# Reordering the two MLP products of a float32 transformer block on one core: DVE's other work between the splits, slices with their high and low parts in one piece each

## The chip, the core and the metric

The kernel runs on one core of one Trainium2 chip. The metric is device time in microseconds (us): the median of three runs, with a profile of one further execution. TensorE (PE) multiplies, VectorE (DVE) and ScalarE (ACT) prepare its operands and finish its results, SyncE (SP) issues most loads, GpSimd (Pool) issues the transfers that add in memory. SP, ACT and Pool each have a DMA queue; in the profile they are q1, q10 and q0.

## What is computed

One layer of a streaming encoder in float32: RMSNorm, an input projection, two kinds of attention, gates, an output projection, and then an MLP of hidden width 8192 for 512 tokens of width 2048. The change is in the MLP alone:

```
h2 = rms_norm(x, norm_mlp[layer])
u = jax.nn.relu(h2 @ w_mlp_up[layer])
x = x + (u * u) @ w_mlp_down[layer]
```

## The kernel before

**Numbers in two parts.** A float32 operand is split into a high part, rounded to PE's fast float32 format (ACT, an activation with Copy), and a low part, the rest (DVE, a subtraction). A product is three matmuls: high by high, high by low, low by high.

**Seven products instead of eight.** Both MLP products multiply 2 x 2 blocks by a scheme of the Strassen and Winograd kind with seven products. DVE first makes sums of blocks of weights (L1425, L1428, L1430, one call `sum_pairs` for the weights of two units), and combines the seven results afterwards (`combine_early`, L1445 to L1451, and `combine_late`, L1458) once ACT has copied one of them (`copy_p1`, L892).

**Units.** A unit is two slices of activations by a pair of weight tiles: 2 x 7 x 3 = 42 matmuls. It needs the weights' high part (`round_pair`, ACT L887) and low part (`split_pair`, DVE L1435). There are two buffers for these parts, so `round_pair` of unit n waits until PE has finished unit n - 2. Four weight buffers `pairs[0..3]` hold raw weights and sums.

**The up product** has 32 pairs of columns p, four units each. A loop over i takes two pairs: m = 0 to 3 is one, m = 4 to 7 the next, with the results in two sets of PSUM banks. The results of one pair are combined at m = 1 or m = 5 of the next. ACT then squares them (`finish_pair`), DVE makes the sums that the down product needs (`sum_u`, L1677 to L1683), and ACT stores them as one row block of `u_rows` in device memory, seven tiles of 256 columns (`store_u`).

**The down product** has 32 groups g of four units j = 0 to 3: eight column blocks by four windows of the hidden width. Group g uses the eight slices g to g + 7, of which each next group exchanges one; slice e lies in buffer e modulo 8. `load_slice` brings it back (SP, L601), `round_slice` (ACT, L1119) and `split_slice` (DVE, L1722) split it. The loads, as SP issues them:

```
for g in range(GROUPS):
    for j in range(4):
        load_down(g, j)          # waits until pair_lo_ready says that buffer j is free
        ...
        if g > 0 and j == 1 and g + 7 < EVENTS:
            load_slice(g + 7)
```

PE waits before every unit for `pair_lo_ready` (the split of the weights), and in the down product for `slice_ready` of the slices up to g + 2j + 1. For the first 24 groups Pool stores the combined results into `sum_rows` (from the ninth group on with addition). In the last eight (`CLOSING` = 24 and up) DVE adds the stored sums (`total`), PE transposes ahead of unit j = 3 of the next group (`turn_out`, L2119), ACT scales from PSUM into `out_tok` (`scale_out`, four activations, L1126), and Pool adds `out_tok` to the output in memory (`add_out`). `scale_out` waits until `out_tok` is free again, `at_least(act, out_added, 16 * (g - CLOSING))`, and PE's group g + 2 waits for `scale_out` of g.

**Order.** Each engine runs its own list, written out by hand; semaphores tie the lists together. A waiting instruction holds up everything behind it on its engine. In `up_pairs` and in the loops over g, each engine's list says in which place of a unit a side task stands; the change is mostly about these places. On DVE, before: at unit 1 (and 5) `combine_early`, `split_pair`, `combine_late`; after `split_pair` of each even unit the next `sum_pairs`. On ACT, before: at unit 1 (and 5) `copy_p1` and then `round_pair`.

**Slices in SBUF.** A slice buffer is 7 tiles x 2 parts x 256 columns: high and low part of a tile stand side by side. The load fills the low part's place, in seven pieces of 1 KB per row, and both parts are then made from there. The up product uses the same buffers for its eight slices of the normed input.

## Time and profile before

| | us |
|---|---|
| median of 3 runs | 2810.18 |
| lowest, highest | 2807.93, 2812.83 |
| the profiled execution | 2803.63 |
| its span, first to last instruction | 2801.9 |
| PE busy in the span | 2677.7 |
| DVE busy | 1990.3 |
| ACT busy | 1204.7 |
| mean granted TensorE clock | 0.993 of full speed |

The up product runs from 1350 us to 2038 us of the span, the down product from 2044 us to 2784 us. PE is counted busy while a matmul is under way, so the difference to a stretch's length is time in which PE had nothing to do. L numbers are lines of the kernel.

### The profile page before, as it was taken

To read this page: it belongs to the slowest core of one execution; us is meant where nothing else is said; L and a number is where in the kernel's file an instruction comes from. 1 tells how busy PE (TensorE), PEld (TensorE's weight loads), DVE (VectorE), ACT (ScalarE), POOL (GpSimd) and SP (SyncE) were. 2 spreads that over 40 slices of the span, in tenths; PEclk is the share of its full clock that TensorE was granted. 3 is DMA by queue.
4 is the path that set the end of the run, shared out by engine and by line. 5 is a ranking of instruction groups with operands and counts; after the bars stand their busy time and mean duration, and the time that the engine had idled before them with its cause. 6 is when DMAs were issued, how large, how long until landed. Compare 5 with 4: busy or idle time off the path is not lost.

```text
span 2801.9 us, 48322 instructions
## 1 busy us (share of the span) xinstructions
PE 2677.7 (96%) x18330; PEld 2484.5 (89%) x18330; DVE 1990.3 (71%) x3081; ACT 1204.7 (43%) x1539; POOL 74.2 (3%) x100
## 2 busy tenths in 40 slices
PE   9999999999999999999999999999979989988997
PEld 8999999888888888888999999999979988888897
DVE  4558886777777644434777787777788777777775
ACT  5534444555554532233444444444453333333443
POOL 0000000000010000000000000000000000000000
PEclk9999999999999999999999999999989999999999
DMA  6444444333233254434344444443474555555564
GB/s 242 125 124 136 127 135 123 84 83 79 75 79 82 84 144 138 144 125 158 111 137 137 150 137 143 136 151 131 149 230 157 167 148 155 159 159 154 170 175 104
DMA packets 396462, 381.43 MB, mean 136 GB/s; under 512 B 18368, under 2 KB 380480, under 8 KB 395840
## 3 DMA queue, kind: packets, MB, share of 16 engines
q1 hardware_dynamic: 366352, 311.73, 36.6%
q10 hardware_dynamic: 21168, 47.19, 4.5%
q0 software_dynamic: 8832, 20.97, 4.0%
q8 instruction: 77, 1.26, 0.2%
q14 instruction: 33, 0.27, 0.0%
HBM read 316.91 MB, written 62.91 MB: 136 GB/s over the span
## 4 chain that ended last, share of the span: by engine, by line
PE 56%; DVE 20%; DMA 11%; issue 6%; ACT 5%; SPq 1%; ACTq 0%; DVEq 0%; POOL 0%
DMA h<-u_rows 8%; DVE lo L1435 7%; PE job L1777 7%; PE job L1780 7%; PE job L1779 7%; ACT hi L887 3%; DVE pair L1425 3%; DVE h L1722 2%; DMA pair<-in_w_mlp_up 2%; DVE pair L1428 2%; ACT h L1119 2%; DVE blocks L1445 1%; PE heads_out L1877 1%; PE job L2090 1%; DVE pair L1430 1%
## 5 line engine op out<-in xcount | busy, mean ns | idle before, releaser
L887 ACT ACTIVATE hi<-pair 128x1792 fp32r<-128x1792 f32 x270 | 458.5, 1698 | 600.1 <-PE wide L2094 269.3
L1435 DVE TENSOR_TENSOR lo<-pair,hi 128x1792 fp32r<-128x1792 f32 x270 | 545.8, 2022 | 141.0 <-ACT hi L887 140.9
L2090 PE MATMUL scores<-h,hi 128*128 128x256 f32 x1024 | 297.2, 290 | 62.9 <-DVE lo L1435 62.9
L2090 PE MATMUL job<-h,hi 128*128 128x256 f32 x1024 | 294.1, 287 | 41.7 <-DVE lo L1435 41.7
L722 ACT ACTIVATE w_hi<-raw 128x512 fp32r<-128x512 f32 x268 | 168.8, 631 | 353.9 <-PE job L1780 242.9
L1175 DVE TENSOR_TENSOR w_lo<-raw,w_hi 128x512 fp32r<-128x512 f32 x268 | 187.1, 699 | 158.2 <-ACT w_hi L722 157.2
L2094 PE MATMUL scores<-h,lo 128*128 128x256 f32 x1024 | 291.8, 285 | 0.0
L2092 PE MATMUL scores<-h,hi 128*128 128x256 f32 x1024 | 291.5, 285 | 0.0
L2094 PE MATMUL job<-h,lo 128*128 128x256 f32 x1024 | 290.0, 283 | 0.0
L2092 PE MATMUL job<-h,hi 128*128 128x256 f32 x1024 | 289.9, 283 | 0.0
L2090 PEld LDWEIGHTS scores<-h,hi 128*128 128x128 f32 x1024 | 197.9, 193 | 71.7 <-issue 47.7
L2090 PEld LDWEIGHTS job<-h,hi 128*128 128x128 f32 x1024 | 196.3, 192 | 50.3 <-issue 40.0
L1777 PE MATMUL job<-a_hi,w_hi 128*128 128x512 f32 x560 | 229.5, 410 | 0.0
L1780 PE MATMUL job<-a_hi,w_lo 128*128 128x512 f32 x560 | 219.6, 392 | 0.0
L1779 PE MATMUL job<-a_lo,w_hi 128*128 128x512 f32 x560 | 218.6, 390 | 0.0
L1425 DVE TENSOR_TENSOR pair<-pair 128x1024 f32<-128x1024 f32 x128 | 156.5, 1222 | 82.4 <-DMA pair<-in_w_mlp_down 57.5
L2092 PEld LDWEIGHTS scores<-h,hi 128*128 128x128 f32 x1024 | 198.1, 194 | 0.0
L2094 PEld LDWEIGHTS scores<-h,lo 128*128 128x128 f32 x1024 | 198.1, 193 | 0.0
L2094 PEld LDWEIGHTS job<-h,lo 128*128 128x128 f32 x1024 | 196.5, 192 | 0.0
L2092 PEld LDWEIGHTS job<-h,hi 128*128 128x128 f32 x1024 | 196.5, 192 | 0.0
L2090 PE MATMUL turned<-h,hi 128*128 128x256 f32 x512 | 146.0, 285 | 0.0
L2092 PE MATMUL turned<-h,hi 128*128 128x256 f32 x512 | 146.0, 285 | 0.0
(458 smaller groups left out, 7025.8 us busy)
## 6 DMA issues: line engine op xcount, KB each, us to landing
pair<-in_w_mlp_up SPq DMA_DIRECT2D x256, 256.0 KB, 2.8
pair<-in_w_mlp_down SPq DMA_DIRECT2D x248, 256.0 KB, 3.3
raw<-in_w_in SPq DMA_DIRECT2D x79, 512.0 KB, 4.1
h<-u_rows SPq DMA_DIRECT2D x39, 896.0 KB, 9.0
u_rows<-u_blocks ACTq DMA_DIRECT2D x32, 896.0 KB, 4.1
pair<-in_w_gate SPq DMA_DIRECT2D x84, 256.0 KB, 2.9
raw<-in_w_out SPq DMA_DIRECT2D x64, 256.0 KB, 3.3
sum_rows<-blocks POOLq DMA_DIRECT2D x24, 512.0 KB, 7.4
```

What stands on the lines that cost most here:

```text
L722: nc.scalar.activation(into, raw[:, slot, part:part + KU], ACT.Copy).then_inc(hi_ready, 1)
L887: nc.scalar.activation(pair_hi[j % 2], pairs[j][:, :, 1:8], ACT.Copy).then_inc(pair_hi_ready, 1)
L1119: nc.scalar.activation(slot[:, :, 0], slot[:, :, 1].bitcast(F32), ACT.Copy).then_inc(slice_hi, 1)
L1175: nc.vector.tensor_tensor(lo, raw[:, slot, part:part + KU], hi.bitcast(F32), ALU.subtract).then_inc(split_ready, 1)
L1425: nc.vector.tensor_tensor(t[:, :, 4:6], t[:, :, 1:3], t[:, :, 0:1].broadcast_to([P, 4, 2, P]), ALU.add).then_inc(sums_first, 2)
L1435: nc.vector.tensor_tensor(pair_lo[j % 2], pairs[j][:, :, 1:8], pair_hi[j % 2].bitcast(F32), ALU.subtract).then_inc(pair_lo_ready, 1)
L1777: nc.tensor.matmul(result[:, :], high[:, k], act_hi[:, f], start=(n == 0 and k == 0), stop=False)
L1779: nc.tensor.matmul(result[:, :], high[:, k], act_lo[:, f], start=False, stop=False)
L1780: done = nc.tensor.matmul(result[:, :], low[:, k], act_hi[:, f], start=False, stop=(n == units - 1 and k == KU - 1))
L2090: nc.tensor.matmul(into, high, h_slices[s][:, a, 0], start=first, stop=False, skip_group_check=True)
L2092: nc.tensor.matmul(into, high, h_slices[s][:, a, 1], start=False, stop=False, skip_group_check=True)
L2094: done = nc.tensor.matmul(into, low, h_slices[s][:, a, 0], start=False, stop=(j == 3 and k == 1), skip_group_check=True)
```

## The change

DVE and ACT do their side tasks in another place: at each unit the split of weights (and ACT's rounding for it) comes first, and then one other task. In the down product the slices' buffers are seen as two contiguous parts, high and low, through `slots`, and PE reads them through `down_slice`; the load then writes one piece of 7 KB per row. The up product keeps the old layout. In the first group the splits of slices 4 to 7 stand one place later than before, one or two at a time. `scale_out` of a group moves from unit 3 of the group after it to unit 0 of the one after that, behind `round_pair`.

```diff
             out_tok = over(third, "out_tok", [P, TB, 2 * P])
+
+        slots = [[t.rearrange("p a l s -> p (a l s)")[:, 7 * 2 * P * l:7 * 2 * P * (l + 1)] for l in range(2)]
+                 for t in h_slices]
+
+        def down_slice(e, a, l):
+
+            return slots[e % 8][l][:, 2 * P * a:2 * P * (a + 1)]
...
                 sp.wait_ge(u_stored, 16 * (e % PAIRS + 1))
-                sp.dma_start(h_slices[e % 8][:, :, 1].bitcast(F32),
-                             u_rows[e % PAIRS].rearrange("p (a s) -> p a s", a=7)).then_inc(slice_loaded[e % 8], 16)
+                sp.dma_start(slots[e % 8][1].bitcast(F32), u_rows[e % PAIRS]).then_inc(slice_loaded[e % 8], 16)
...
                     n = i * 8 + (GU + m)
-                    if m == 0 and not first:
-                        store_u(i * 2 - 2)
+                    if not (first and m < 4):
+                        round_pair(n, m % 4, n - 1)
                     if m == 1 and not first:
...
                         copy_p1(i * 2 + GP, 0, blocks)
-                    if not (first and m < 4):
-                        round_pair(n, m % 4, n - 1)
+                    if m == 0 and not first:
+                        store_u(i * 2 - 2)
                     if m == 2 and not first:
...
                 act.wait_ge(slice_loaded[e % 8], 16 * (e // 8 + 1))
-                slot = h_slices[e % 8]
-                nc.scalar.activation(slot[:, :, 0], slot[:, :, 1].bitcast(F32), ACT.Copy).then_inc(slice_hi, 1)
+                hi, lo = slots[e % 8]
+                nc.scalar.activation(hi, lo.bitcast(F32), ACT.Copy).then_inc(slice_hi, 1)
...
                     n = down_unit(g, j)
+                    round_pair(n, j, n - 1)
+                    if j == 0:
+                        if g < 2:
+                            store_u(PAIRS - 2 + g)
+                        if g == CLOSING + 2:
+                            act.wait_ge(r2_ready, 1)
+                            act.wait_ge(u_stored, 16 * PAIRS)
+                        if g >= CLOSING + 2:
+                            scale_out(g - 2)
                     if j == 1:
...
                         copy_p1(GP + PAIRS + g - 1, (g - 1) % 2, blocks)
-                    round_pair(n, j, n - 1)
                     if g == 0 and j == 0:
-                        store_u(PAIRS - 2)
-                    if g == 0 and j < 3:
-                        round_slice(2 * j + 2)
-                        round_slice(2 * j + 3)
+                        round_slice(2)
+                        round_slice(3)
+                    if g == 0 and j == 1:
+                        round_slice(4)
+                        round_slice(5)
                     if g == 0 and j == 2:
                         finish_pair(PAIRS - 1)
-                    if g == 1 and j == 0:
-                        store_u(PAIRS - 1)
-                    if j == 3:
-                        if g + 8 < EVENTS:
-                            round_slice(g + 8)
-                        if g == CLOSING:
-                            act.wait_ge(r2_ready, 1)
-                            act.wait_ge(u_stored, 16 * PAIRS)
-                        if g > CLOSING:
-                            scale_out(g - 1)
+                        round_slice(6)
+                        round_slice(7)
+                    if j == 3 and g + 8 < EVENTS:
+                        round_slice(g + 8)
             act.wait_ge(total_ready, GROUPS - 1 - CLOSING)
             copy_p1(GP + PAIRS + GROUPS - 1, (GROUPS - 1) % 2, blocks)
+            scale_out(GROUPS - 2)
             scale_out(GROUPS - 1)
...
                         continue
+                    split_pair(n, m % 4)
                     if m == 1:
                         combine_early(i * 2 + (GP - 1), 1, blocks)
+                        combine_late(i * 2 + (GP - 1), 1, blocks)
                     if m == 5:
                         combine_early(i * 2 + GP, 0, blocks)
-                    split_pair(n, m % 4)
-                    if m == 1:
-                        combine_late(i * 2 + (GP - 1), 1, blocks)
-                    if m == 5:
                         combine_late(i * 2 + GP, 0, blocks)
...
                 dve.wait_ge(slice_hi, e + 1)
-                slot = h_slices[e % 8]
-                nc.vector.tensor_tensor(slot[:, :, 1], slot[:, :, 1].bitcast(F32), slot[:, :, 0].bitcast(F32),
-                                        ALU.subtract).then_inc(slice_ready, 1)
+                hi, lo = slots[e % 8]
+                nc.vector.tensor_tensor(lo, lo.bitcast(F32), hi.bitcast(F32), ALU.subtract).then_inc(slice_ready, 1)
...
                     n = down_unit(g, j)
+                    split_pair(n, j)
+                    if g == 0 and j == 1:
+                        split_slice(4)
                     if j == 1:
                         combine_early(p, (g - 1) % 2, blocks)
-                    split_pair(n, j)
-                    if j == 1:
                         combine_late(p, (g - 1) % 2, blocks)
...
                             total(g - 1)
-                    if g == 0 and j < 3:
-                        split_slice(2 * j + 2)
-                        split_slice(2 * j + 3)
+                    if g == 0 and j == 2:
+                        split_slice(5)
                     if j % 2 == 0 and n + 2 < down_unit(GROUPS, 0):
                         sum_pairs(n + 2, (j + 2) % 4)
-                    if j == 3:
-                        if g == 0:
-                            sum_u(PAIRS - 1)
-                        if g + 8 < EVENTS:
-                            split_slice(g + 8)
+                    if g == 0 and j == 0:
+                        split_slice(2)
+                        split_slice(3)
+                    if g == 0 and j == 3:
+                        split_slice(6)
+                        split_slice(7)
+                        sum_u(PAIRS - 1)
+                    if j == 3 and g + 8 < EVENTS:
+                        split_slice(g + 8)
             combine_early(GP + PAIRS + GROUPS - 1, (GROUPS - 1) % 2, blocks)
...
-            def up_unit(n, j, b, slices_wait=False, at=0):
+            def up_slice(s, a, l):
+
+                return h_slices[s][:, a, l]
+
+            def up_unit(n, j, b, slices_wait=False, at=0, slice_of=up_slice):
...
                 for k in range(2):
-                    s = (at + 2 * j + k) % 8
+                    s = at + 2 * j + k
                     if slices_wait:
...
                         first = j == 0 and k == 0 and half == 0
-                        nc.tensor.matmul(into, high, h_slices[s][:, a, 0], start=first, stop=False,
+                        nc.tensor.matmul(into, high, slice_of(s, a, 0), start=first, stop=False,
                                          skip_group_check=True)
-                        nc.tensor.matmul(into, high, h_slices[s][:, a, 1], start=False, stop=False,
+                        nc.tensor.matmul(into, high, slice_of(s, a, 1), start=False, stop=False,
                                          skip_group_check=True)
-                        done = nc.tensor.matmul(into, low, h_slices[s][:, a, 0], start=False,
+                        done = nc.tensor.matmul(into, low, slice_of(s, a, 0), start=False,
                                                 stop=(j == 3 and k == 1), skip_group_check=True)
...
                     pe.wait_ge(slice_ready, g + 2 * j + 2)
-                    up_unit(down_unit(g, j), j, g % 2, at=g)
+                    up_unit(down_unit(g, j), j, g % 2, at=g, slice_of=down_slice)
             turn_out(GROUPS - 1)
```

## Rows read from the trace of the kernel before

**Rows 1.** Busy time by stage: stretch, us, PE PEld DVE ACT POOL (instructions), PEclk, DMA, GB/s
```profile
1397.30:1995.50 598.20, 572.42 (x4706) 566.52 (x4704) 472.43 (x505) 257.86 (x224) 0.00 (x0) 1.00 0.42 141
1995.50:2099.30 103.80, 87.45 (x671) 86.16 (x670) 85.22 (x81) 50.99 (x39) 0.78 (x1) 0.92 0.62 201
2099.30:2599.40 500.10, 455.11 (x3703) 447.76 (x3701) 380.57 (x354) 191.46 (x134) 16.63 (x22) 1.00 0.55 157
2599.40:2784.30 184.90, 170.76 (x1400) 168.15 (x1400) 141.21 (x138) 76.24 (x73) 14.37 (x16) 1.00 0.59 159
```

**Rows 2.** The chain that ended last, up product: start us, us, what
```profile
1619.20 0.12 PE scores L2094
```

**Rows 3.** Who waited for whom, PE, whole span: us, times, longest us
```profile
PE scores L2090 <- DVE lo L1435: 62.9, 43, 6.2
PE job L2090 <- DVE lo L1435: 41.7, 47, 3.3
```

**Rows 4.** Timeline of ACT, up product: start us, us, what [idle before]
```profile
1611.48 1.69 ACT L887 ACTIVATE hi<-pair 128x1792 fp32r<-128x1792 f32 x1
```

**Rows 5.** Timeline of DVE in the same pair, columns as above
```profile
1613.56 0.69 DVE L1445 TENSOR_TENSOR blocks<-job,blocks 128x512 f32<-128x512 f32 x1
...
1615.55 2.01 DVE L1435 TENSOR_TENSOR lo<-pair,hi 128x1792 fp32r<-128x1792 f32 x1
```

**Rows 6.** Timeline of PE in the same pair
```profile
1617.62 0.39 PE L2090 MATMUL scores<-h,hi 128*128 128x256 f32 x1 [1.36 <-DVE lo L1435]
```

**Rows 7.** The chain that ended last, one down group
```profile
2305.30 1.95 DVE lo L1435
...
2308.24 9.95 DMA h<-u_rows
...
2318.22 1.71 ACT h L1119
...
2319.95 1.65 DVE h L1722
...
2321.89 2.02 DVE lo L1435
...
2328.63 1.94 DVE lo L1435
```

**Rows 8.** DMA queues: packets, MB, share; q1 and q10 from 1500 to 2000, q0 from 2100 to 2600
```profile
q1 hardware_dynamic: 51099, 49.26, 31.4%
q10 hardware_dynamic: 3456, 22.02, 10.6%
...
q0 software_dynamic: 3168, 11.54, 12.5%
```

**Rows 9.** Landings: u_rows 2110:2740 and 1500:2000, in_w_mlp_down 2110:2740, out_tok 2640:2802
```profile
DMA to landing us min/median/max: 7.0/9.1/11.2
...
DMA to landing us min/median/max: 4.0/4.1/4.2
...
DMA to landing us min/median/max: 2.3/3.4/10.6
...
DMA to landing us min/median/max: 5.6/5.9/8.2
```

**Rows 10.** Timeline of Pool, the down group of rows 7
```profile
2307.86 0.85 POOL L676 DMA_DIRECT2D sum_rows<-blocks  x1 [22.79 <-DVE blocks L1458]
```

**Rows 11.** Timeline of ACT at the end
```profile
2784.57 0.38 ACT L892 ACTIVATE blocks<-heads_out 128x256 f32<-128x256 f32 x1 [3.51 <-PE heads_out L2094]
2790.49 1.57 ACT L1126 ACTIVATE out_tok<-job,r 128x256 f32<-128x256 f32 x4 [5.54 <-PE job L2119]
```

**Rows 12.** The chain that ended last, a transposing in the last groups
```profile
2778.57 0.87 PE scores L2119 x8
```

**Rows 13.** Timeline of DVE, first down group
```profile
2048.72 2.03 DVE L1722 TENSOR_TENSOR h<-h 128x1792 fp32r<-128x1792 f32 x1 [2.65 <-ACT h L1119]
```

**Rows 14.** Timeline of PE, first down group
```profile
2072.21 0.36 PE L2090 MATMUL scores<-h,hi 128*128 128x256 f32 x1 [2.28 <-DVE lo L1435]
```

## The prediction

> **What bounds the kernel now.** I read the stages' busy time first, then who waited for whom, then one period of each MLP product on DVE, ACT and PE and as a chain of waits, then the DMA queues and the times to landing.
>
> The stages [rows 1]: the up product's steady part is 28 pairs of columns in 598.2 us, so 21.36 us a pair; the down product's steady part is 22 groups in 500.1 us, 22.7 us a group; the last eight groups take 184.9 us. A pair and a group are both four units of 42 matmuls (two slices, seven products, three matmuls each). The chain steps through them at 0.12 us a matmul [rows 2]: 5.04 us a unit, 20.2 us for four. PE's busy time per up pair is 572.42 / 28 = 20.4 us, which still holds a slow first matmul after each wait. I take 20.3 us as what four units cost when PE never waits. PE is then the bound only in part: 1.1 us of each pair and 2.4 us of each group are waits, and PE waits for one thing in both products, the DVE split of the weights: 62.9 + 41.7 us over the kernel [rows 3].
>
> Why that split is late differs. In the up product ACT has the high part of unit m = 1 from 1611.48 to 1613.17 [rows 4], but DVE, done with its sums at 1613.56, first does the whole of combine_early (L1445 to L1451), so the split starts at 1615.55 [rows 5] and PE waits 1.36 us until 1617.62 [rows 6]. In the down product the same stands before unit j = 1, and a longer loop runs through it [rows 7]: the split of j = 1 ends (2307.25), SP issues two weight loads and then the slice (2308.24), the slice lands 9.95 us later, ACT rounds it, DVE splits it, then splits j = 0, then sums, combines, splits j = 1 (2328.63 + 1.94 = 2330.57). From one such end to the next are 23.3 us. Written as a sum: 1.0 to the issue, L to the landing, 1.73 ACT, 1.94 slice split, 2.02 split of j = 0, 4.72 for sums and combine_early (2321.89 + 2.02 = 2323.91 to 2328.63), 1.94 split. That is 13.35 + L, with L = 9.95 it is 23.3, the measured period. So this loop, and not PE, sets the down product.
>
> **The change, part by part.**
> 1. *The split of unit 1 (and 5) goes ahead of combine_early, and ACT's rounding ahead of copy_p1.* Nothing is added; combine_early is 2.0 us of DVE (1613.56 to 1615.55) [rows 5], copy_p1 a short copy on ACT. Take PE's start of the unit before as 0. ACT's high part is ready at 1.9 us (released by the end of the unit before that), the sums (2.75 us, 4.72 of rows 7 less the combine's 2.0) end at 1.6 if the split ahead of them ended 1.1 us early, the split runs to 3.95, ahead of 5.04. Then both combines (2.4 us) to 6.3, where unit 2's high part comes at 6.9; its split ends at 8.9 of 10.1. Every slot holds one split (1.95 from start to start) and at most the sums: 4.7 of 5.07 us. So in the up product PE's wait should go: 598.2 - 28 x 20.3 = 29.8 us. What hides the combine is the 15 us before its bank is needed again.
> 2. *The same in the down product.* It takes the combine out of the loop: 11.3 + L. This is under 20.3 as long as L is under 9.0 us.
> 3. *High and low part of a slice each in one piece.* The matmuls read the same 256 columns. ACT's and DVE's durations shouldn't change: the weights' split and the slice's split take 2.02 us for the same 1792 elements in different pieces [rows 7] (the 1.65 us there is the part on the chain; the next instruction's start shows 1.94). I give them nothing; both bounds are 0. What changes is the transfer: rows of 7 KB instead of seven pieces of 1 KB. From 1500 to 2000 us q1, all 1 KB pieces, spent 31.4% of 16 x 500 us on 49.26 MB, 51 engine-us per MB; q10, which stores whole slices, 10.6% on 22.02 MB, 38.5 per MB [rows 8]. A slice of 0.9175 MB would need 2.2 us of all engines instead of 2.9. Bounds of L: 4.1 us, what the store of a slice takes, and 9.1 (7.0 to 11.2), what the load takes now [rows 9]. One more thing pulls it down. Pool's store of the sums leaves at 2307.86 [rows 10], 0.4 us ahead of the slice, and costs 12.5% of 8000 engine-us per 11.54 MB, so 2.8 us of all engines for its 0.52 MB [rows 8]. It waits for the combine. With the 2.0 us of combine_early behind the split it leaves 2.6 us after the split's end, the slice 1.0, so 1.6 us ahead. Two weight loads (0.52 MB at 51, 1.7 us) stay ahead: 1.7 + 2.2 + 1.9 (4.1 less 2.2) = 5.8, and some sharing. I take L = 6.5. Then the loop is 17.8 us, under 20.3, and PE bounds the down product: 500.1 - 22 x 20.3 = 53.5 us saved.
> 4. *scale_out after the next round_pair, one group later.* In the last eight groups the rounding of j = 0 stood behind four activations of 1.57 us together [rows 11]; now they stand behind it, with PE's unit j = 3 to cover them. PE's own floor is 8 x 20.3 + 7 x 0.9 (the transposes [rows 12]) = 168.7 of 184.9 us: 16.2 us saved. total adds two instructions of 512 elements, some 1.2 us, to DVE's slot of j = 1, 1.95 + 2.4 + 1.2 = 5.5 us and so over one unit; but the slot starts 1.1 us ahead, and DVE is busy 141.21 / 8 = 17.7 of 21.2 us [rows 1].
> 5. *First group's order.* The stretch from 1995.5 to 2099.3 holds two pairs and two groups: 103.8 - 81.2 = 22.6 us over the floor. Of that 2.1 is part 1. The rest is eight slices of 0.92 MB that come only as the up product lets go of their buffers, and then DVE's work: it stands 2.65 us for the slice that it splits at 2048.72 [rows 13], and goes on until PE can start unit 3 at 2072.21 [rows 14]. The new order leaves all of that work; it fills the 2.65 us with the sums, and the shorter transfers bring slices 0 and 1 some 1 us sooner. But unit 2 now waits for slice 5 behind the combine and its own split. I take 3 us besides the 2.1, between -5 and 13.
> 6. *The end.* The last scale_out but one moves behind the last copy_p1. out_tok must be free before the last scale_out, so that now waits for a transfer: PE ends just ahead of the last copy_p1 at 2784.57, which ends at 2784.95 [rows 11], scale_out to 2786.6, Pool's addition lands 5.9 us after its issue [rows 9], 2792.6, against 2790.49 before [rows 11]: 2.1 us lost (1.8 to 4.4 with landings of 5.6 and 8.2).
>
> At one place a rule speaks against part 3. The Trainium skill, DMA: Bandwidth & Descriptors, section Specifications, has pieces of 512 B and more at line rate; by it 1 KB pieces gain nothing from being longer. The rows (51 against 38.5 engine-us per MB) disagree, though they compare a load with a store. By the rule alone L would stay near 9.1 and the case below marked A follows. The same page, section Queues, rings and completion order, has each DMA engine take turns between queues packet by packet; by that a slice in longer packets would also get a larger share beside Pool's store. No row shows this.
>
> **Sum.** 29.8 + 53.5 + 16.2 + 5.1 - 2.1 = 102.5 us. Of this I leave 5.5 us as waits that stay in a period with 0.4 to 1.1 us of slack (late weight loads, stray clock losses): 97 us. The profiled execution took 2803.63 us (span 2801.9 and 1.7 around it), so it would be 2706.6; the median of the runs is 6.5 us above it, so 2810.2 - 97 = 2713 us.
>
> **Rivals.**
> *A. Transfers stay the bound of the down product.* L stays at 9.1 to 11.2 us because pieces of 1 KB were no burden. For it: of L's 9.1 us only 2.9 are the slice's own. Against it: the store moves behind it. The loop is 20.4 to 22.5 us; at L = 9.9 it is 21.2, so 0.9 us a group stay lost in 23 groups (the last eight last 21.2 anyway), 21 us, and 4 more in the first group's transfers: 2738 us.
> *B. Only the up product and the split order gain.* The weight loads' landing has a median of 3.4 but a longest of 10.6 us [rows 9], and DVE waits in order for them: sums before split 1 tolerate 5.6 us after the issue. If slices in front of them in SP's queue and the store take turns so that DVE stands 1.5 us in each group, 31 x 1.5 = 46 us are lost: 2759 us.
> *C. Slower.* The same place, with one price: the loads for j = 2 and 3 are issued 6 us before their sums must start; the sums stand ahead of split 1, so every microsecond beyond 5.6 from issue to landing stops PE in each of some 62 pairs and groups. To undo 97 us and add 6 it takes 103 / 62 = 1.7 us each, landings at 7.3 us. The median is 3.4 [rows 9], and nothing is added to the traffic; at 7.5 us it would be 2713 + 62 x 1.9 = 2831 us.
> *D. No change.* PE's waits are replaced by equal ones in another unit. Against it: DVE's busy time is 472.43 / 28 = 16.9 us a pair and 380.57 / 22 = 17.3 us a group [rows 1], under 20.3. 2810 us.
>
> **Chances.** Forecast (2698 to 2725) 0.66, A 0.17, B 0.11, C 0.03, D 0.02, and 0.01 for something faster than 2698. Range: the forecast's own and A's, up to 2742, leaves some 0.17 out; downwards the first group's better bound and no leftover give 2713 - 5.5 - 10 = 2697.5. So 2697 to 2742. What measurement can tell from no change is 0.2%, 5.6 us: faster 0.95, same 0.02, slower 0.03.
>
> **What the profile after would show.** In the up product no PE wait on the split, pairs of 20.3 us, each split of m = 1 ahead of L1445. In the down product groups near 20.3 us, slices landing within 8 us, the ACT wait for the slice no longer followed by a PE wait. In the last eight groups 21.2 us each. At the end scale_out waiting for Pool's transfer. Wrong would be: slice landings over 9 us, DVE waiting for weight loads longer than 2 us ahead of split 1, or a lower granted clock in the long stretches without a wait.

## The result and the profile after

The changed kernel takes 2695.4 us (median of 4 runs, 2694.2 to 2697.1), the kernel before in the same series 2809.1 us (4 runs, 2805.8 to 2812.8): a ratio of 0.9595, with a 95% interval of 0.9579 to 0.9612. That is 113.7 us off where 97 were predicted, and 1.6 us below the low end of the range. The profiled execution took 2696.0 us with a span of 2694.2, so the spans differ by 107.7 us.

Busy time by stage of the changed kernel, one row for each row of [rows 1] and one for the end (stretch, us, PE PEld DVE ACT POOL, PEclk, DMA, GB/s):
```profile
1397.40:1961.90 564.50, 564.50 (x4706) 564.50 (x4705) 472.63 (x506) 257.09 (x224) 0.00 (x0) 1.00 0.44 150
1961.90:2061.10 99.20, 86.54 (x675) 85.78 (x674) 85.45 (x81) 50.95 (x39) 0.78 (x1) 0.93 0.60 211
2061.10:2504.60 443.50, 443.50 (x3698) 443.50 (x3697) 383.61 (x353) 193.19 (x132) 16.64 (x22) 1.00 0.62 177
2504.60:2674.60 170.00, 168.86 (x1410) 168.36 (x1409) 140.39 (x137) 75.59 (x70) 13.08 (x15) 1.00 0.63 172
2674.60:2694.20 19.60, 2.01 (x9) 1.57 (x8) 3.67 (x7) 3.41 (x9) 2.60 (x2) 0.60 0.39 54
```
The borders of these stretches and of those in [rows 1] don't fall on the same matmul in both traces (3703 and 3698 records, 1400 and 1410). Counted instead from ACT's timeline, from the moment at which the end of a pair or a group releases ACT (before 1397.52, 1995.80, 2100.15, 2598.75 and 2784.57, changed 1398.71, 1963.19, 2062.35, 2505.87 and 2674.74), in us:

| | ahead of them | 28 up pairs | 2 pairs, 2 groups | 22 groups | last 8 groups | end |
|---|---|---|---|---|---|---|
| before | 1397.5 | 598.3 | 104.4 | 498.6 | 185.8 | 17.3 |
| changed | 1398.7 | 564.5 | 99.2 | 443.5 | 168.9 | 19.5 |
| gain | -1.2 | 33.8 | 5.2 | 55.1 | 17.0 | -2.1 |

"Released" below means this way of counting.

In both steady parts PE's busy time is the whole stretch, 564.50 of 564.50 and 443.50 of 443.50 us: 28 pairs at 20.16 us and 22 groups at 20.16. That is 168 matmuls of 0.12 us, with nothing between them. DVE's busy time in the same parts is that of before within 1% (472.63 against 472.43, 383.61 against 380.57): DVE's work did not become cheaper.

The page's busy time and its chain that ended last:
```profile
PE 2656.4 (99%) x18330; PEld 2478.9 (92%) x18330; DVE 1992.6 (74%) x3081; ACT 1206.2 (45%) x1539; POOL 74.2 (3%) x100
...
PE 96%; DVE 2%; DMA 1%; ACT 1%; issue 0%; SPq 0%; POOL 0%; ACTq 0%; DVEq 0%
```
The chain of the kernel before, by its page:
```profile
PE 56%; DVE 20%; DMA 11%; issue 6%; ACT 5%; SPq 1%; ACTq 0%; DVEq 0%; POOL 0%
```
PE is now the bound in both products, but not at their border (86.54 us busy of 99.20) nor at the end. What it still waits for in the two products (PE, whole span: us, times, longest), where [rows 3] had 62.9 and 41.7 us:
```profile
PE scores L2105 <- DVE lo L1445: 6.6, 2, 5.2
PE scores L2105 <- DVE h L1730: 6.1, 2, 3.8
PE job L2105 <- DVE lo L1445: 4.5, 3, 3.3
```
Of these the first two lines are the first group, 3.3 us the start of the up product, and 1.1 us two waits in the last eight groups.

DVE in one down group, from the split of unit j = 0 to that of j = 3 (start us, us, what, idle before):
```profile
2260.64 2.03 DVE L1445 TENSOR_TENSOR lo<-pair,hi 128x1792 fp32r<-128x1792 f32 x1 [0.80 <-ACT hi L893]
2262.59 1.22 DVE L1435 TENSOR_TENSOR pair<-pair 128x1024 f32<-128x1024 f32 x1
...
2265.68 2.03 DVE L1445 TENSOR_TENSOR lo<-pair,hi 128x1792 fp32r<-128x1792 f32 x1 [0.28 <-ACT hi L893]
2267.63 0.68 DVE L1455 TENSOR_TENSOR blocks<-job,blocks 128x512 f32<-128x512 f32 x1
...
2269.61 0.41 DVE L1468 TENSOR_TENSOR blocks<-blocks,stats 128x256 f32<-128x256 f32 x1
2270.73 2.03 DVE L1445 TENSOR_TENSOR lo<-pair,hi 128x1792 fp32r<-128x1792 f32 x1 [0.70 <-ACT hi L893]
...
2275.76 2.02 DVE L1445 TENSOR_TENSOR lo<-pair,hi 128x1792 fp32r<-128x1792 f32 x1 [0.29 <-ACT hi L893]
2278.43 2.02 DVE L1730 TENSOR_TENSOR h<-h 128x1792 fp32r<-128x1792 f32 x1 [0.65 <-ACT h L1125]
```
The splits start at 2260.64, 2265.68, 2270.73 and 2275.76, one in each 5.04 us of PE. Between two of them stand the sums, or both combines (L1455 to L1468), or the slice's split, and before each of them in this group DVE waits for ACT, with 0.3 to 0.8 us to spare. In [rows 5] and [rows 7] a combine stood between the sums and a split. ACT's high part, in turn, is released by PE, and for the slice it waits 0.97 us of DMA, which now costs PE nothing (ACT, SP's queue and Pool in the same group):
```profile
2268.99 1.71 ACT L893 ACTIVATE hi<-pair 128x1792 fp32r<-128x1792 f32 x1 [3.07 <-PE wide L2109]
...
2276.70 1.70 ACT L1125 ACTIVATE h<-h 128x1792 fp32r<-128x1792 f32 x1 [0.97 <-DMA h<-u_rows]
```
```profile
2268.92 0.34 SPq L608 DMA_DIRECT2D h<-u_rows  x1
```
```profile
2270.32 0.85 POOL L682 DMA_DIRECT2D sum_rows<-blocks  x1 [19.31 <-DVE blocks L1468]
```
The slice leaves 1.4 us ahead of Pool's store, where [rows 10] had the store 0.4 us ahead; 1.6 was worked out. The landings of slices, and below them of the down product's weights, from 2070 to 2630, beside the medians of [rows 9] (9.1 and 3.4 us):
```profile
DMA to landing us min/median/max: 6.6/7.3/8.5
```
```profile
DMA to landing us min/median/max: 2.3/3.3/8.5
```
L, the time from the slice's issue to its landing, has a median of 7.3 us, not 6.5; the longest, 8.5, is still under the 9.0 at which the loop would take over.

ACT at the end, beside [rows 11]:
```profile
2674.74 0.38 ACT L898 ACTIVATE blocks<-heads_out 128x256 f32<-128x256 f32 x1 [9.23 <-PE heads_out L2109]
2675.02 1.56 ACT L1132 ACTIVATE out_tok<-scores,r 128x256 f32<-128x256 f32 x4
2682.73 1.57 ACT L1132 ACTIVATE out_tok<-job,r 128x256 f32<-128x256 f32 x4 [6.15 <-DMA out<-out_tok]
```
From the start of the last copy_p1 to that of the last scale_out are 7.99 us, and the latter waits for a transfer; before, they were 5.92 (2790.49 less 2784.57). The 2.1 us of part 6 are there.

### The profile page after: what moved, and what is told of

It reads as the page before. It is cut to its first block, busy times and chain, and to the rows that moved or that the text cites. A ratio compares the mean times of both kernels' runs of the same rounds, so it can differ in the third digit from the quotient of the medians.

```text
span 2694.2 us, 48322 instructions
## 1 busy us (share of the span) xinstructions
PE 2656.4 (99%) x18330; PEld 2478.9 (92%) x18330; DVE 1992.6 (74%) x3081; ACT 1206.2 (45%) x1539; POOL 74.2 (3%) x100
## 3 DMA queue, kind: packets, MB, share of 16 engines
q8 instruction: 77, 1.26, 0.2%
## 4 chain that ended last, share of the span: by engine, by line
PE 96%; DVE 2%; DMA 1%; ACT 1%; issue 0%; SPq 0%; POOL 0%; ACTq 0%; DVEq 0%
PE job L1788 7%; PE job L1791 7%; PE job L1790 7%; PE job L2105 4%; PE job L2107 4%; PE job L2109 4%; PE scores L2105 4%; PE scores L2109 4%; PE scores L2107 4%; PE stats L2107 2%; PE stats L2109 2%; PE stats L2105 2%; PE turned L2105 2%; PE turned L2109 2%; PE turned L2107 2%; PE heads_out L1888 1%
## 5 line engine op out<-in xcount | busy, mean ns | idle before, releaser
L2105 PE MATMUL scores<-h,hi 128*128 128x256 f32 x1024 | 291.9, 285 | 12.7 <-DVE lo L1445 6.6
L2107 PE MATMUL scores<-h,hi 128*128 128x256 f32 x1024 | 290.9, 284 | 0.0
```

The source lines that it names most:

```text
L2105: nc.tensor.matmul(into, high, slice_of(s, a, 0), start=first, stop=False, skip_group_check=True)
L2107: nc.tensor.matmul(into, high, slice_of(s, a, 1), start=False, stop=False, skip_group_check=True)
```

## The experiments

Each ratio is to the kernel before in the same series, whose medians were 2807.4, 2810.0, 2808.4 and 2810.8 us, with its 95% interval. Differences to the changed kernel are between medians of different series.

**One part alone: the up product's new order.** The kernel before, with DVE's and ACT's new lists in the up product only:
```
+                    split_pair(n, m % 4)
                     if m == 1:
                         combine_early(i * 2 + (GP - 1), 1, blocks)
+                        combine_late(i * 2 + (GP - 1), 1, blocks)
...
-                    split_pair(n, m % 4)
-                    if m == 1:
-                        combine_late(i * 2 + (GP - 1), 1, blocks)
...
```


> The up product's lists of DVE and ACT are those of the changed kernel, all else is as before. If the two products gain separately (my theory), the up product's 28 steady pairs fall from 598.2 to 564.5 us and nothing else moves: 34 us off, so about 2775 us, and the down product keeps its 22.7 us a group and the wide scatter from run to run. Rival: part of the gain of one product comes from the other (a shared start, the clock): then it is off by more than 5 us.

Measured 2771.5 us (2767.2 to 2772.0, 4 runs), 0.9876 (0.9860 to 0.9893). The up pairs take 20.16 us each (564.48 us for 28, released), the down groups nearly what they took before (497.1 us for 22). **The other half**, the changed kernel with the up product's lists as before (the same diff, reversed):

> The changed kernel with the up product's lists of DVE and ACT as before. Two questions. Additive or not: the up product's 28 pairs should go back to 598.2 us, 34 us more than the changed kernel: 2729 us. And where the scatter of the kernel before comes from (its runs go from 2803.5 to 2815, its profiled execution took 2803.6): if from the down product's loop, whose length hangs on a landing, the runs of this kernel lie within 3 to 4 us, and its profiled execution is near its median. Rival: the scatter is the chip's, then they go over 7 us or more here too.

Measured 2731.1 us (2729.9 to 2732.6, 4 runs), 0.9728 (0.9712 to 0.9745). Alone the two halves take off 35.9 and 77.3 us, together 113.2, and the whole change takes off 113.7: they add up, and neither needs the other. This run was also to show where the scatter of the kernel before comes from; that is taken up with the step from the profile to the median below.

**Is it the layout?** The changed kernel with each slice back in seven pieces of 1 KB:
```
-        slots = [[t.rearrange("p a l s -> p (a l s)")[:, 7 * 2 * P * l:7 * 2 * P * (l + 1)] for l in range(2)]
-                 for t in h_slices]
+        slots = [[t[:, :, l] for l in range(2)] for t in h_slices]
...
-                sp.dma_start(slots[e % 8][1].bitcast(F32), u_rows[e % PAIRS]).then_inc(slice_loaded[e % 8], 16)
+                sp.dma_start(slots[e % 8][1].bitcast(F32),
+                             u_rows[e % PAIRS].rearrange("p (a s) -> p a s", a=7)).then_inc(slice_loaded[e % 8], 16)
```


> The changed kernel with the slices laid out as before (seven pieces of 1 KB in each row of the load). Theory: the order does it. The loop is 11.3 us + L, and with Pool's store behind the slice L is 8 to 9 us even in pieces of 1 KB, so the loop stays at or just above 20.2 us: 2695 to 2705 us, the most of it in the first group. Rival: the longer pieces carry the down product, L goes back to 9 to 10 us, the loop to 21 us, some 0.9 us a group in 23 groups: 2715 us or more.

Measured 2698.1 us (2697.0 to 2698.9, 4 runs), 0.9613 (0.9597 to 0.9629): 2.7 us above the changed kernel, with intervals of the ratio that overlap. In its trace 1.6 us of the difference arise ahead of the 28 up pairs, where nothing differs; its 22 down groups take 1.4 us more (444.87 against 443.52, released), the stretch with the first group 1.5 more and the last eight groups 1.6 less. And the kernel before with the new layout alone (that diff on the kernel before, the other way round):

> The kernel before with only the new layout of the slices. Theory: the loop keeps combine_early and is 13.35 us + L, L falls by 0.7 to 2 us, the period goes from 22.7 us towards 21.4 us, of which the wait before unit 1 (1.5 us) stays in any case: 16 to 30 us off in the down product, nothing in the up product, 2780 to 2793 us. Rival: a transfer that is hidden anyway gives nothing without the order, 2809 us.

Measured 2805.4 us (2802.7 to 2812.8, 10 runs), 0.9998 (0.9988 to 1.0008): nothing, against an expectation of 16 us and more. Landings in its trace from 2150 to 2500, of slices and then of Pool's store (the kernel before has medians of 9.4 and 7.3 us in that stretch):
```profile
DMA to landing us min/median/max: 7.0/9.7/10.3
```
```profile
DMA to landing us min/median/max: 7.1/10.3/10.8
```
Longer pieces did not bring the slice in sooner while Pool's store left just ahead of it; the store itself landed later. So the order carries the gain; the layout is worth at most some 3 us with it, which these runs hardly resolve, and nothing that shows without. Nor did q1 spend 38.5 engine-us per MB on the slices, as the prediction took over from the stores. By its share and MB from 2100 to 2500 it spent 50.5 in the kernel before and 50.2 with the layout alone, 52.1 with the order alone and 51.3 with both, where slices at 38.5 would have taken about 4 off.

**Which lists carry the order?** The changed kernel with ACT's lists as before in both products:
```
-                    if not (first and m < 4):
-                        round_pair(n, m % 4, n - 1)
+                    if m == 0 and not first:
+                        store_u(i * 2 - 2)
                     if m == 1 and not first:
                         copy_p1(i * 2 + (GP - 1), 1, blocks)
                     if m == 5:
                         copy_p1(i * 2 + GP, 0, blocks)
-                    if m == 0 and not first:
-                        store_u(i * 2 - 2)
+                    if not (first and m < 4):
+                        round_pair(n, m % 4, n - 1)
...
```


> The changed kernel with ACT's lists as before: copy_p1 ahead of the rounding at units 1 and 5, the store of u ahead of it at unit 0, scale_out at unit 3 of the next group. Theory: the order on DVE carries the gain. copy_p1 is released by the same event as the rounding and makes it 0.3 us later, the slack is 1.1 us, so nothing is lost in the steady parts; the last eight groups lose at most 0.5 us each, the end gains back 2.1 us: 2693 to 2698 us. Rival: ACT's order is half of the gain, 2705 us or more.

Measured 2697.5 us (2697.2 to 2702.8, 4 runs), 0.9610 (0.9583 to 0.9638). The steady parts lose little (40.39 us for two up pairs against 40.32). Six of the last eight groups take 21.88 us instead of 21.02, all eight 4.7 us more (173.6 against 168.9, released), and the end gets back 1.6. The medians show only 2.1 us of this; in the profiled executions PE reached the 28 up pairs 2.8 us earlier than in the changed kernel, at a granted clock of 1.00 from 1350 to 1400 us against 0.93. So ACT's order is worth some 4 us by the traces, and DVE's order carries the rest. No run has DVE's new order entirely by itself; each of the others was taken away alone. **The first group's places as before:**
```
...
-                        round_slice(2)
-                        round_slice(3)
...
+                    if g == 0 and j < 3:
+                        round_slice(2 * j + 2)
+                        round_slice(2 * j + 3)
```
with DVE's split_slice calls likewise.

> The changed kernel with the first group's slices rounded and split in the old places (4 and 5 after unit 1, 6 and 7 after unit 2, ahead of the sums). Theory: the stretch around the first group is bound by DVE's work and the transfers, which are the same, so it is 0 to 4 us slower: 2695 to 2699 us. Rival: the new places are what took the 4.6 us off there, and more is lost through the clock: 2700 us or more.

Measured 2694.4 us (2692.2 to 2698.5, 4 runs), 0.9605 (0.9589 to 0.9621): the new places there are worth nothing that shows (98.5 us in its trace for the two pairs and two groups, against 99.2). What part 5 gained came with the rest: the layout alone brings that stretch from 104.4 to 102.9 us.

**The slot model: does place decide, or work?** DVE is idle 3.3 us in each up pair of the changed kernel (472.63 / 28 = 16.9 of 20.16). One more subtraction of 2.0 us was put ahead of the split of units 1 and 5, into a slot that already holds the sums:
```
+                    if m % 4 == 1:
+                        dve.wait_ge(pair_hi_ready, n + 1)
+                        nc.vector.tensor_tensor(pair_lo[m % 2], pairs[m % 4][:, :, 1:8], pair_hi[m % 2].bitcast(F32),
+                                                ALU.subtract).then_inc(twice, 1)
+                        dve.wait_ge(twice, i * 2 + m // 4)
                     split_pair(n, m % 4)
```


> The changed kernel with one more subtraction of 2.0 us on DVE ahead of the split of units 1 and 5 of the up product (the same operands, done twice). Theory: a slot holds one split and 3 us of other work, and only that; in this one the sums (2.75 us) come first, so the split ends 6.1 us after PE's start of the unit before and PE waits 1.0 us and refills: 1.15 us in each of 30 pairs, 35 us, 2730 us, although DVE then is busy 19 of 20.2 us. Rival: DVE is idle 3.3 us a pair and takes it up: no change.

Measured 2729.0 us (2728.5 to 2731.8, 4 runs), 0.9719 (0.9693 to 0.9745): 33.6 us above the changed kernel; in its trace the 28 up pairs take 32.4 us more (released), 1.16 each. DVE and PE's waits in its trace:
```profile
1613.21 2.02 DVE L1706 TENSOR_TENSOR lo<-pair,hi 128x1792 fp32r<-128x1792 f32 x1 [0.29 <-ACT hi L893]
1615.27 2.03 DVE L1445 TENSOR_TENSOR lo<-pair,hi 128x1792 fp32r<-128x1792 f32 x1
```
```profile
PE scores L2112 <- DVE lo L1445: 19.5, 17, 4.8
PE job L2112 <- DVE lo L1445: 17.6, 17, 3.3
```
From the start of the sums, 1610.11 in the same timeline, to the split's end are now 7.2 us, over 2 more than a slot of 5.04. In the changed kernel the split was done 1.3 us before PE came to it (2265.68 + 2.03 against ACT's release by PE at 2268.99); what goes beyond that lead, about 1 us, PE waits: 29 waits more than in the changed kernel, with 26.0 us (37.1 less 11.1), 0.9 each, and some 0.3 us each to get going again. DVE has 18.9 us of work in a pair, less than 20.16, and the wait is back all the same. What has to fit is each slot, not the pair.

**How late may the slice be?** The changed kernel with one number in SP's list changed: the slice behind the weight loads of the next unit.
```
-                    if g > 0 and j == 1 and g + 7 < EVENTS:
+                    if g > 0 and j == 2 and g + 7 < EVENTS:
                         load_slice(g + 7)
```


> The changed kernel with the slice's load one place later in SP's list, behind the weight loads of unit 2 instead of unit 1. Theory (the loop): it then runs from the split of unit 2: 1.0 us to the issue, L, 1.73, 1.94, 2.02, and 9.1 us for sums, the split of unit 1, the combine and the split of unit 2, so 15.8 us + L, and with L = 7.3 it is 23.1 us, 2.9 us over PE's 20.16 in 22 to 23 groups: 65 us more, 2760 us; between 2745 and 2775 us as L is 6.6 to 8. Rival: L was never what bound it, the slice has a whole group to come, no change.

Measured 2804.9 us (2797.8 to 2810.7, 10 runs), 0.9986 (0.9976 to 0.9996): the whole gain gone, 109.6 us, where 50 to 80 were expected. The chain and PE's timeline in one group, then its stretches:
```profile
2346.80 7.05 DMA h<-u_rows
2353.88 1.71 ACT h L1125
2355.61 1.65 DVE h L1730
2357.26 0.29 issue
2357.56 2.03 DVE lo L1445
```
```profile
2356.73 0.28 PE L2109 MATMUL heads_out<-h,lo 128*128 128x256 f32 x1
2359.72 0.35 PE L2105 MATMUL scores<-h,hi 128*128 128x256 f32 x1 [2.71 <-DVE lo L1445]
...
2361.28 0.41 PE L2109 MATMUL scores<-h,lo 128*128 128x256 f32 x1
2361.50 0.41 PE L2105 MATMUL scores<-h,hi 128*128 128x256 f32 x1
```
```profile
2359.40:2366.60 7.20, 6.88 (x45) 6.91 (x46) 6.91 (x10) 0.03 (x1) 0.00 (x0) 0.76 0.39 123
...
2064.00:2599.00 535.00, 474.68 (x3697) 470.89 (x3697) 380.37 (x354) 189.41 (x132) 16.65 (x22) 0.94 0.49 147
```
Two things make a group of 24.4 us (536.5 / 22, released; the last eight take 192.7 us). PE waits 2.7 us for the split behind the slice, as the loop has it; and then its matmuls step by 0.21 us instead of 0.12, at a mean granted clock of 0.76 in that stretch, so at the lower level of 1.2 GHz in part of it. That second part was not foreseen. In the 22 groups PE waits 62.6 us in 23 pieces, the longest 4.4, and the groups take 93.0 us more than the changed kernel's: 1.3 us beside each wait. In the kernel before, PE waited 44.2 us in that part, in 38 pieces of at most 2.6 us, the clock stayed at 1.00 [rows 1], and the groups took 55.1 us more: 0.3 us beside each wait. The Trainium skill (TensorE: Matmul & The Clock Gate, Part 1: The HAM clock gate) has the clock follow how busy PE has been lately. These two traces agree with that in direction, 0.94 with the long waits and 1.00 with the short ones. **The same with slices in seven pieces:**

> The late slice with the slices laid out in seven pieces of 1 KB. In this kernel every microsecond of L shows in the time, 23 times. If a slice in long pieces lands sooner by its bytes (51 against 38.5 engine-us per MB: 0.7 us), it is 16 us slower than the late slice with the new layout. If the other transfers around it take up the difference, as without the new order, it is within 6 us of it.

Measured 2832.5 us (2828.6 to 2849.2, 4 runs), 1.0101 (1.0063 to 1.0139), 27.6 us above the one before it, where 16 were expected. The landings' medians are 7.1 (new layout) and 7.6 us, PE's waits from 2064 to 2599 us 62.6 and 70.5 us, the mean clock there 0.94 and 0.93. The spans are 23.6 us apart. Released, 9.1 of that are in the 22 groups, 11.2 in the last eight, where PE's waits grow from 19.2 to 25.5 us, and 3.2 in the stretch with the first group. So with the slice on the path the longer pieces pay, by more than the 0.5 us of the median landing; how the rest comes about is open.

**The end and the first group.** The changed kernel with the last scale_out but one put at unit 3 of the last group:
```
+                    if j == 3 and g == GROUPS - 1:
+                        scale_out(g - 1)
             act.wait_ge(total_ready, GROUPS - 1 - CLOSING)
             copy_p1(GP + PAIRS + GROUPS - 1, (GROUPS - 1) % 2, blocks)
-            scale_out(GROUPS - 2)
             scale_out(GROUPS - 1)
```


> The changed kernel with the last scale_out but one back at unit 3 of the last group. Theory: the last scale_out no longer waits for Pool's transfer (it began 8.2 us after PE's end instead of 6.1): 2.1 us off, 2693 us. Rival: the transfers at the end are served one after the other in either order, no change.

Measured 2695.1 us (2693.0 to 2697.1, 4 runs), 0.9598 (0.9572 to 0.9624). In the trace copy_p1 to scale_out takes 6.32 us (2673.36 to 2679.68), 1.7 less than in the changed kernel; the medians do not resolve it. The longer end of the changed kernel is thus shown in the trace, not in the time. One more edit on top, slices 0 to 3 in SP's queue ahead of the weight loads of units 2 and 3:
```
-                    load_down(g, j)
                     if g == 0 and j > 1:
                         load_slice(2 * j - 4)
                         load_slice(2 * j - 3)
+                    load_down(g, j)
```


> As the kernel with the end put back, and in SP's list slices 0 to 3 ahead of the weight loads of units 2 and 3 of the first group. Theory: slices 0 and 1 are let go by PE 5 us before SP now comes to them, since it waits for the weight buffer of unit 2; issued 4 to 5 us sooner, PE's wait of 5.2 us at the start of the down product goes, DVE is the bound of what follows: 4 to 7 us off, 2686 to 2689 us. Rival: the weight loads behind them come late by as much, and units 2 and 3 lose it again: no change against the kernel with the end put back.

Measured 2691.5 us (2691.0 to 2691.7, 4 runs), 0.9582 (0.9557 to 0.9607), 3.9 us under the changed kernel. PE's wait ahead of the first unit falls from 5.16 to 1.26 us; that ahead of the next grows from 1.39 to 6.00, because the weights are now the late ones: DVE waits 2.64 us for them ahead of its sums. So all eight slices early, in DVE's first group the splits and the sums ahead of the combine, and ACT's finish_pair one unit later:

> The kernel with the early slices, and slices 4 to 7 ahead of the weight loads of the next group too; DVE's first group in the order split, two slices, with the sums behind the split of unit 1 and the combine behind that of unit 3. Theory: in the kernel with the early slices DVE stood 2.6 us for the weights of units 2 and 3 ahead of slices that had landed, and ACT 5.2 us for slice 4; with both gone DVE's work (27.5 us from PE's start of the group) is all that is left, so the second group starts some 6 us sooner: 2685 us. Rival: the transfers are the bound, 3.7 MB of slices and 2 MB of weights in 16 us, and the waits move: 2690 us or more.

Measured 2692.9 us (2691.6 to 2694.5, 4 runs), 0.9589 (0.9573 to 0.9605). The rival's number came, by another mechanism. ACT in its trace:
```profile
2033.12 0.63 ACT L1087 ACTIVATE u_blocks<-blocks 128x512 f32<-128x512 f32 x1 [10.20 <-DVE blocks L1470]
```
The work on the last pair's sums (finish_pair) stood in ACT's queue for the combine that had been moved back, and behind it the rounding of the next group's weights: PE then waited 7.6 us in one piece. With it behind that rounding, and the store and sum_u that follow it later too:
```
+                    if g == 1 and j == 0:
+                        finish_pair(PAIRS - 1)
+                    if g == 1 and j == 2:
+                        store_u(PAIRS - 1)
...
-                        finish_pair(PAIRS - 1)
```


> As the kernel with all slices early, and ACT's squares of the last pair (which wait for DVE's combine) behind the rounding for the second group's first unit instead of ahead of it, with what follows from them (sum_u, the store) in the second group. Theory: the reorder of the first group did bring units 0 to 3 forward (unit 3 began 4 us sooner), and one wait on ACT, placed ahead of that rounding, gave it back (7.8 us before unit 0 of the second group). With it gone that wait is about 2 us: 2687 us, 6 us under the kernel with all slices early. Rival: the DMA queues, at 420 GB/s in this stretch, are the bound, then the wait turns up elsewhere and it is 2691 us or more.

Measured 2687.3 us (2685.7 to 2688.8, 4 runs), 0.9559 (0.9543 to 0.9575), as expected. ACT's wait at that place in its trace:
```profile
2029.98 0.63 ACT L1087 ACTIVATE u_blocks<-blocks 128x512 f32<-128x512 f32 x1 [0.62 <-DVE blocks L1472]
```
10.20 us have become 0.62. It is the fastest version, 8.1 us under the changed kernel; in its trace 5.3 us of that are in the stretch with the first group (93.9 us, released) and 2.0 at the end.

## Why the prediction was right in its steps and wrong in its sum

The mechanism held in the two products and at the end. The sum came out too small: it took four units of PE at 20.3 us instead of 20.16, it kept 5.5 us for waits that did not come, and the median was carried over from a profiled execution that lay low.

- **Part 1, up product:** 29.8 us predicted, 33.8 measured (released). **Part 2 and 3, down product:** 53.5 and 55.1. **Part 4, last eight groups:** 16.2 and 17.0, with 1.1 us of small waits left. **Part 5, first group:** 5.1 and 5.2; the number is right by luck, since the new places that it was given to are worth nothing. **Part 6, the end:** 2.1 lost in both. Ahead of the up pairs 1.2 us were lost, where nothing was changed and no term stood. Sum 102.5 and 107.7.
- **The step that failed** is "I take 20.3 us as what four units cost when PE never waits". It was taken from PE's busy time with waits in it (20.4), instead of from the chain's own step [rows 2]: 168 x 0.12 = 20.16. Once PE doesn't wait there is no slow first matmul either. Over 28 + 22 periods that is 7.0 us, and 1.1 more in the last eight groups. Parts 1 to 4 miss by 6.4 us together, so it more than covers that miss; the stretch of 500.1 us that part 3 started from also holds some 1.5 us more than 22 groups (498.6).
- **The leftover of 5.5 us** "as waits that stay in a period" was a guess without a row, and no such wait is there (PE busy for all of both stretches). It covered the same waits as the margin in the 20.3 a second time, and made 97 us of what is 107.7. The low end of the range took back the leftover but not the 20.3, and the measured time lies 1.6 us below it.
- **From profiled execution to median.** I carried over that the median lies 6.5 us above the profiled execution. After, it lies 0.6 below it. That is 7.1 of the 17.8 us between 2713.2 and 2695.4; the sum is the other 10.7. The kernel before may repeat less well because its period hung on DMA landings (7.0 to 11.2 us). For it: the kernel with only the new down product, which was expected to keep within 3 to 4 us if so, spread over 2.7 us in 4 runs with its profiled execution 1.2 below the median; the one with only the new up product, which keeps the loop, over 4.8 in 4; 13 runs of the kernel before over 10.8, and the late slice, whose loop hangs on landings too, over 12.9 in 10. Four runs are few, so this is made likely, not shown.
- **L:** 6.5 us predicted, 7.3 measured (7.9 with the old layout, a loop of 19.2 and still under 20.16; its longest, 9.7, is over). The price did not matter, as part 2 had it: under 9.0 PE is the bound. Of the shortening, the order is the larger share: 9.1 to 7.9 by order, 7.9 to 7.3 by pieces. The term "2.2 us of all engines instead of 2.9" for the slice came from comparing a load with a store and did not hold: q1's time per MB hardly fell. That the pieces would bring the slice in sooner by themselves was wrong in the kernel before (experiment with the layout alone).
- **Rival A** had slices at 9.1 us or more and fell with them. **Rivals B and C** needed weight loads that stop DVE: their median stayed at 3.3 us, and DVE waited 2.9 us in all for the down product's and 0.7 for the up product's. **Rival D** fell with PE's busy time. The slot reasoning that speaks against D is borne out by the doubled split: DVE had 3.3 us free, and 2.0 us in the wrong slot cost 1.16 a pair. The sign of being wrong that looked at the clock did not appear either: 1.00 in both steady parts.
- **The rule weighed in part 3.** The Trainium skill (DMA: Bandwidth & Descriptors, Specifications) holds 1 KB pieces to be at full rate already. The runs lie between it and the prediction. Nothing that shows in the kernel before, at most some 3 us in the changed one, and the queue's time per MB (50.5 and 50.2, 52.1 and 51.3) agree with it; the landings (7.9 to 7.3) and the 27.6 us with a late slice, where the time per MB falls from 51.5 to 49.1, do not.

## What to carry to other kernels

Where an engine feeds PE once per unit, divide its list by those units and fit each slot: what PE waits for comes first in its slot, everything else behind it, in all queues on that path. For the time that remains when PE no longer waits, multiply matmuls by the chain's own step; don't use PE's busy time of a stretch with waits, and don't keep a reserve that no row shows. When work is moved back on one engine, look in the other engines' queues for what waits for it, and for what stands behind that.

## What the runs showed that was not expected

- The clock's price of a wait is no fixed one. With a late slice PE waits 2.8 us a group, matmuls after the wait shown stepped by 0.21 us, and the mean clock was 0.94; with the shorter waits of the kernel before the mean stayed at 1.00. And near the start of the up product PE waits 3.3 us at the same place in every trace looked at; from 1373.7 to 1387.0 the granted clock is 0.74 in the changed kernel's trace and 1.00 in that with the new end:
```profile
1373.70:1387.00 13.30, 11.20 (x73) 11.23 (x74) 10.31 (x11) 5.08 (x6) 0.00 (x0) 0.74 0.25 79
```
```profile
1373.70:1387.00 13.30, 9.99 (x83) 9.81 (x83) 11.30 (x12) 7.11 (x7) 0.00 (x0) 1.00 0.25 79
```
  From the end of this wait (1375.80 and 1377.36) to the start of the 28 up pairs (1398.71 and 1397.78) are 22.9 and 20.4 us: 2.5 us from one run to another, without any difference in the code there. It is as large as several of the effects that were looked for at the end and in the first group.
- Seven pieces or one made no difference to ACT and DVE: the split of 1792 elements takes 2.02 us in both layouts, and ACT's rounding 1.70 us.
- With the slice in long pieces, Pool's store just ahead of it landed later (a median of 10.3 us against 7.3 from 2150 to 2500), and the slice no sooner (9.7 against 9.4). Whether the queues' sharing does that was not tried.
